# Block 2's decay: masked copies ahead of weight splits and convolutions, subtractions on GpSimd, exponentials over half tiles

## The reference, cut to what matters

```python
f = lb + (1.0 - lb) * jax.nn.sigmoid(f_raw)
log_f = jnp.log(f)
k = 1.0 - f
...
G = jnp.cumsum(lfc, axis=2)
diff = G[:, :, :, None, :] - G[:, :, None, :, :]
decay = jnp.where(mask, jnp.exp(jnp.minimum(diff, 0.0)), 0.0)
scores = jnp.einsum('bhtk,bhsk,bhtsk->bhts', qc, kc, decay)
```

## Time and profile before

| | us |
|---|---|
| median of 3 runs | 2746.95 (2746.0, 2746.95, 2749.92) |
| span of the profiled execution, first to last instruction | 2750.0 |
| PE busy in the span | 2545.7 (93%) |
| DVE busy | 1340.7 (49%) |
| ACT busy | 914.7 (33%) |
| GpSimd busy | 230.3 (8%) |

### The profile page before, as it was taken

The page is one execution under the profiler, slowest core; times in us unless marked ns, Lnnn a source line. Parts: engine busy times, 40 slices in busy tenths (PEclk is TensorE's granted clock), DMA queues, the critical chain, the costliest instruction groups (busy, mean ns, idle before and its releaser), DMA issues. The chain is left out here.

```text
span 2750.0 us, 39357 instructions
## 1 busy us (share of the span) xinstructions
PE 2545.7 (93%) x16728; PEld 1799.5 (65%) x16728; DVE 1340.7 (49%) x1877; ACT 914.7 (33%) x1236; POOL 230.3 (8%) x160
## 2 busy tenths in 40 slices
PE   7979899998999899678999899999999999999998
PEld 6652333332333333277799799899799899897897
DVE  4541122211212222277777665756575665765755
ACT  4431111110111111144454444444344444425443
POOL 2000000000000000000000011253020100102300
PEclk9989999999999999887899999999999999989999
DMA  9668999999999999942355466455466466441462
GB/s 322 235 239 365 427 428 403 427 428 427 427 400 426 427 427 427 364 127 92 108 193 194 163 212 211 157 177 191 153 223 209 154 209 205 139 156 35 166 205 101
DMA packets 248701, 713.71 MB, mean 260 GB/s; under 512 B 12531, under 2 KB 186313, under 8 KB 223622
## 3 DMA queue, kind: packets, MB, share of 16 engines
q1 hardware_dynamic: 237136, 690.26, 65.7%
q10 hardware_dynamic: 9734, 17.02, 1.8%
q0 software_dynamic: 1648, 3.82, 0.4%
HBM read 710.01 MB, written 1.05 MB: 259 GB/s over the span
## 5 line engine op out<-in xcount | busy, mean ns | idle before, releaser
L365 DVE TENSOR_TENSOR lo<-ring,hi 128x2048 fp32r<-128x2048 f32 x251 | 597.4, 2384 | 298.9 <-ACT hi L356 298.8
L356 ACT ACTIVATE hi<-ring 128x2048 fp32r<-128x2048 f32 x251 | 476.3, 1900 | 151.1 <-PE bank L653 116.2
L2014 PE MATMUL bank<-expert,xg 128*64 128x512 f32 x1664 | 393.7, 612 | 43.4 <-DMA expert<-in_w_mlp 42.2
L423 PE MATMUL bank<-x_hi,hi 128*128 128x256 f32 x1568 | 367.3, 279 | 0.0
L423 PE MATMUL bank<-x_lo,hi 128*128 128x256 f32 x1568 | 364.6, 278 | 0.0
L423 PEld LDWEIGHTS bank<-x_hi,hi 128*128 128x128 f32 x1568 | 295.1, 188 | 3.2 <-issue 1.6
L423 PEld LDWEIGHTS bank<-x_lo,hi 128*128 128x128 f32 x1568 | 294.9, 188 | 2.5 <-issue 1.0
L2014 PEld LDWEIGHTS bank<-expert,xg 128*64 128x64 f32 x1664 | 115.7, 139 | 257.8 <-issue 228.1
L2141 DVE TENSOR_TENSOR acc<-bank,acc 128x512 f32<-128x512 f32 x104 | 64.6, 684 | 329.4 <-PE bank L2122 329.4
L428 PE MATMUL bank<-x_hi,lo 128*128 128x256 f32 x1568 | 195.8, 277 | 0.6 <-DVE lo L365 0.6
L2097 PE MATMUL bank<-expert,aT 128*64 128x512 f32 x832 | 186.7, 600 | 5.6 <-DMA expert<-in_w_mlp 4.5
(11 more groups left out here) (650 smaller groups left out, 3776.8 us busy)
## 6 DMA issues: line engine op xcount, KB each, us to landing
expert<-in_w_mlp SPq DMA_DIRECT2D x192, 2048.0 KB, 18.8
ring<-in_l_ffn_w_in SPq DMA_DIRECT2D x88, 1024.0 KB, 5.0
ring<-in_l_ffn_w_out SPq DMA_DIRECT2D x44, 1024.0 KB, 4.8
ring<-in_w_ada SPq DMA_DIRECT2D x24, 1024.0 KB, 6.9
ring<-in_l_gm_w_in SPq DMA_DIRECT2D x24, 1024.0 KB, 5.2
ring<-in_ffn_w_up SPq DMA_DIRECT2D x22, 1024.0 KB, 5.0
ring<-in_w_in SPq DMA_DIRECT2D x21, 1024.0 KB, 7.2
ring<-in_l_gm_w_out SPq DMA_DIRECT2D x12, 1024.0 KB, 4.7
```

Of the source, the lines that this page charges most:

```text
L356: e.activation(k.half("hi", u), k.slot(j), ACT.Copy).then_inc(*k.up("hi_done"))
L365: e.tensor_tensor(k.half("lo", u), k.slot(k.units[u][0]), k.half("hi", u).bitcast(F32), SUB).then_inc(*k.up("lo_done"))
L423: e.matmul(o, l, r, start=fresh, stop=False, skip_group_check=True)
L2014: i = e.matmul(banks[n][j][h * CAP:(h + 1) * CAP, :], x, W[:, (2 * h + j) * 512:(2 * h + j + 1) * 512], start=c == 0, stop=False, skip_gro ...
```

## The change

- DVE's iteration li is now: the two multiplications for level li, copies(li-1), `between_dve(li)`.
- The eight differences are taken on GpSimd, by a new function `decay_less_pool`. The one of level li may start when DVE is through with the multiplications of level li-2, whose `hgE` buffer it takes.
- ACT makes exp(-x) of the lower half and exp(x) of the upper half of every block, two instructions over 384 columns each, with no absolute value ahead of them.
- Before a tanh at level 6, ACT waits for its own instructions.

```diff
+def decay_less_pool(k, e, nm, n):
+
+    e.wait_ge(*k.dve(nm, "sums"))
+    for li in range(1, 9):
+        h = LEVELS[li]
+        nb, r, v = decay_views(k, nm, n, h)
+        P, E = v(k.t[f"{nm}P{r}"]), v(k.t[f"{nm}E{li % 2}"])
+        if li >= 3:
+            e.wait_ge(*k.dve(nm, "level", li - 2))
+        e.tensor_tensor(E, P, P[:, :, h - 1:h].to_broadcast([128, nb, 2 * h]), SUB).then_inc(*k.POOL(nm, "E", li))
...
-    e.wait_ge(*k.dve())
+    k.mark("dve_done", nm, "sums")
     for li in range(10):
-        if li < 8:
-            h = LEVELS[li + 1]
-            nb, r, v = decay_views(k, nm, n, h)
-            P, E = v(k.t[f"{nm}P{r}"]), v(k.t[f"{nm}E{(li + 1) % 2}"])
-            e.wait_ge(*k.dve())
-            e.tensor_tensor(E, P, P[:, :, h - 1:h].to_broadcast([128, nb, 2 * h]), SUB).then_inc(*k.DVE(nm, "E", li + 1))
         if 0 < li < 9:
...
-        if between and li < 9:
-            between(k, e, li)
         if li > 0:
...
                     e.copy_predicated(out[:, :, 0:3:2, :], mask, bank[:, 0:w * 256].rearrange("p (c b s) -> p c b s", c=w, b=2)).then_inc(*k.DVE(*key, frees=key))
...
+        if between and li < 9:
+            between(k, e, li)
...
+def decay_act(k, e, nm, n, between=None):
     for li in range(9):
         if li < 8:
-            E = k.t[f"{nm}E{(li + 1) % 2}"]
-            e.wait_ge(*k.dve(nm, "E", li + 1))
-            e.activation(E, E, ACT.Abs).then_inc(*k.ACT())
-            e.wait_ge(*k.act())
-            e.activation(E, E, ACT.Exp, scale=-1.0).then_inc(*k.ACT(nm, "E", li + 1))
+            h = LEVELS[li + 1]
+            E = decay_views(k, nm, n, h)[2](k.t[f"{nm}E{(li + 1) % 2}"])
+            e.wait_ge(*k.pool(nm, "E", li + 1))
+            e.activation(E[:, :, 0:h], E[:, :, 0:h], ACT.Exp, scale=-1.0).then_inc(*k.ACT())
+            e.activation(E[:, :, h:2 * h], E[:, :, h:2 * h], ACT.Exp).then_inc(*k.ACT(nm, "E", li + 1))
```

More of the change, by code:

```diff
@@ L813, in decay_dve @@
                     e.copy_predicated(out[:, :, 0:3:2, :], mask, bank[:, 0:w * 256].rearrange("p (c b s) -> p c b s", c=w, b=2)).then_inc(*k.DVE(*key, frees=key))
-def decay_act(k, e, nm, between=None):
+        if between and li < 9:
+            between(k, e, li)
+def decay_act(k, e, nm, n, between=None):
     for li in range(9):
         if li < 8:
-            E = k.t[f"{nm}E{(li + 1) % 2}"]
-            e.wait_ge(*k.dve(nm, "E", li + 1))
-            e.activation(E, E, ACT.Abs).then_inc(*k.ACT())
-            e.wait_ge(*k.act())
-            e.activation(E, E, ACT.Exp, scale=-1.0).then_inc(*k.ACT(nm, "E", li + 1))
+            h = LEVELS[li + 1]
[3 more added lines that the diff above has]
+            e.activation(E[:, :, h:2 * h], E[:, :, h:2 * h], ACT.Exp).then_inc(*k.ACT(nm, "E", li + 1))
         if between:
@@ L2533, in block2_act @@
     z_unit_act(k, e, 4)
-    decay_act(k, e, "hg", between_act)
+    decay_act(k, e, "hg", 3, between_act)
     for c in range(3):
@@ L2578, in between_act @@
     elif li == 6:
+        e.wait_ge(*k.act())
         e.activation(t["gth"], t["z"][:, 15:18, :], ACT.Tanh, scale=0.5).then_inc(*k.ACT("hg", "g"))
@@ L3911, in program_pool @@
     decay_pool(k, e, "hg", k.t["hS"])
+    decay_less_pool(k, e, "hg", 3)
     for n in ("mix2", "fin2"):
```

## The result

The changed kernel takes 2729.35 us as the median of 4 runs (2724.34 to 2735.28), the kernel before 2748.43 (2746.0 to 2752.16, 4 runs). The ratio is 0.9927 with a 95% interval of 0.9911 to 0.9943: it is faster, by 19.1 us or 0.7%. The forecast was 19 us faster, 2728 us, in a range of 2723 to 2736. That the two differences agree to 0.1 us is partly luck: the interval of the ratio stands for anything from 15.7 to 24.5 us, and the levels, for which the sum was made, gained 2 us more than the sum. The profiled execution of the changed kernel has a span of 2727.6 us and took 2729.38.

The account below looks back on a forecast made before the run. It took PE's stalls in the decay levels, waiting on DVE and ACT, and the slow clock as the bound; 8.9 + 6.1 + 3.7 = 18.7, say 19 us, took 2746.95 to 2728 us, range 2723 to 2736.

Parts of the forecast that it names:

- z10: PE unit in the levels: with no stall before it, keeps 2.4 GHz and takes 8.2 us instead of 14.3, 6.1 gained.
- The first term: PE from the start of the levels to z10: z10 starts 8.9 us earlier, net of new waits and slow clock.
- the wait before scores(2): PE at level 2: waits 2.1 us for DVE's multiplications, which stand behind a weight unit and the convolution.
- the slow clock in scores(2): PE at level 2: clock falls after the wait, so scores(2) take 3.9 us instead of 2.1, 1.8 lost.
- The clock at level 2: PE after the 2.1 us wait: clock falls, costing 1.8 us in scores(2) and 1.5 in z8.
- the fall seen after 1.18 us: PE in the kernel before: clock fell right after the 1.18 us stall in scores(4), taken as evidence against the rival.
- the rival: Clock stays up at level 2 because the 2.1 us wait is short: 3.3 us less lost, 2725 us; chance 0.14.
- the stall in scores(4): PE: the 1.18 us stall, right after which the clock fell and z10 took 14.3 us, would be gone.
- The median row: GpSimd subtract-like row of 128x1024, median 4.32 us beside DVE work; scaled to 3.2 us as the difference's upper end.
- the copies would not be hit: DVE's masked copies read PSUM and one mask, so GpSimd's differences cost them nothing; up to 1.8 us for copies(0) otherwise.
- The chain behind z10: ACT and DVE from z10's end to scores(7): 3.7 us less, from absolute value 0.75, difference 0.95, copies 2.0.
- The wait that ACT got: ACT's wait for its own instructions, after scores(7): costs 0.1 us at most, covered by its wait for the scans.

Follow-up runs that it names:

- spread: Changed kernel with the convolution's first chunk left at level 1 and the other two moved to level 2; 2724.27 us, levels 69.1 us.
- stall4: Changed kernel with one added PE wait, ahead of the last group of scores(4), for the exponentials of level 6; 2735.64 us, levels 79.3 us.
- no_move: Changed kernel with the order of the copies put back as in the kernel before; 2738.69 us, levels 81.4 us.
- pool_twice: Changed kernel with each difference taken twice on GpSimd, a wait between; 2732.71 us, levels 75.0 us.
- move_halves: Changed kernel with the differences left on DVE, keeping the new copy order and half exponentials; 2730.9 us, levels 74.9 us.
- move_only: Kernel before with only the order changed, masked copies ahead of the weight unit and convolution; 2734.56 us, levels 80.4 us.
- tail: Changed kernel with ACT's square root and GELU moved behind the exponentials of level 7 and the next unit's rounding; 2723.51 us, levels 69.1 us.

## Why the prediction was right, point by point

**The sum.** It was 8.9 + 6.1 + 3.7 = 18.7 us in the levels. In the profiles, each counted from its own end of the scans, z10 starts 11.1 us earlier (40.3 instead of 51.4), takes 5.9 less (8.4 instead of 14.3), and from its end to scores(7) it is 3.65 less (16.2 instead of 19.9): 20.7. From scores(7) to `hS` both kernels take 7.65.

**The first term was 2.2 us too small**, in three parts that nearly explain it. scores(2) ran at 2.4 GHz after all (2.1 us, 3.9 were booked), which is 1.8. z7 started 12.5 us earlier instead of 11.65, as the slow clock at z5 ended 1.7 us sooner in this execution, which is worth half of that. Against that the wait before scores(2) was 2.70 us instead of 2.1, for the same reason: PE came earlier, DVE did not. So the term that was mis-sized is the slow clock in scores(2), booked at 1.8 us and absent.

**The clock at level 2.** I had weighed the rule of the Trainium skill (TensorE: Matmul & The Clock Gate, Part 1), by which a wait of this size keeps the clock, against the fall seen after 1.18 us, and went with the row. The clock did fall, and z8 lost its 1.5 us, but scores(2) did not. So the rival had one half of its 3.3 us. spread, where the wait is gone, kept the clock, but stall4 kept it as well, behind a wait of 2.54 us. From the start of scores(2) to that of scores(3) it takes 10.3 us in stall4 and in the three profiles with the convolution spread, and 11.9 us in each of the five profiles with waits from 2.45 to 4.02 us. Such a wait mostly costs 1.6 us of slow clock and sometimes nothing; its length alone does not settle it, and what does stays open.

**z10.** The cause that I named, the stall in scores(4), was only argued from the order of events, and "right after" was not exact: z10 ran at full pace for its first 1.7 us. stall4 shows that such a stall is enough, with all else as in the changed kernel.

**GpSimd.** The difference took 1.48 us; I had taken 1.8, with 1.4 as one end. The median row was the wrong neighbour for it, as it stood beside DVE work with two SBUF inputs; beside L365 in no_move the same difference took 3.49 us, near my upper end of 3.2. That the copies would not be hit was right, and pool_twice shows it with differences that outlast them (2.00 us again). It shows as well what a collision on the shared way to SBUF costs, 1.0 us on L365. The advice of the Trainium skill (GPSIMD Engine Reference, 4.1 Engine selection) to leave elementwise work on VectorE would have cost time here: GpSimd is 0.5 us slower with each difference, and the levels are 2.4 us shorter than in move_halves, since only the first one is waited for. Of the 2.4 us, 1.4 come ahead of z10 and 1.0 behind it.

**The chain behind z10** was 3.65 us shorter where 3.7 were booked, and its three terms hold one by one: 1.8 us for the copies (move_only against before, 2.0 booked), 0.9 for the exponentials (move_halves against move_only, 0.75) and 1.0 for the difference (changed against move_halves, 0.95). tail shows that the two table loads and functions that I had named hold 3.4 us of what is left.

**The wait that ACT got** is not on the path: ACT waits 4.3 us for the scans a few rows later.

**Where I was wrong** in the experiments was no_move: I had a stall in scores(4) that did not come, as I had moved copies(3) by the convolution's rows and forgot the difference taken off each level of DVE.

## What to carry to other kernels

Where engines run fixed programs and PSUM banks rotate, put what frees a bank ahead of everything that only fills time: here a 2 us copy behind 8 us of other work cost PE 9.6 us. A short stall of PE can cost more than its length, since the unit behind it may run at half clock (6.4 us behind a stall of 1.46 us in stall4, but nothing behind one of 2.54 us in the same execution): look at the granted clock before and after each stall, and at how long the same unit takes elsewhere in the trace. To compare versions that differ by 0.2%, compare the changed stretch between two fixed events in the profiles, as it repeated to 0.1 and 0.6 us in the two kernels that were profiled twice, whose spans differed by 12.1 and 5.1 us.

## What the runs showed of the hardware that I had not expected

- After the stall of 2.70 us before scores(2), the clock stayed at 2.4 GHz for the whole of scores(2) and fell to 1.2 GHz when z8 began. After 4.70 us (move_only) it was at 1.2 GHz for all of scores(2), 3.94 us. After 2.54 us (stall4) it did not fall at all.
- z10 began at 2.4 GHz, fell to 1.2 after 1.7 us (before) and 1.0 us (stall4), and never returned in the rest of its 14.3 and 14.8 us with PE busy throughout, while other units that began slow (z7 and z11 before, z8 in the changed kernel) returned after 3 to 4 us. z10 is the unit with matmuls of 128 columns among those of 256; no run here shows whether that is the reason.
- After a stall of 7.5 to 9.0 us ahead of z5, scores(1) began 7.7 to 9.2 us after the scans in the executions in which they did not wait for DVE, so the return of the clock alone moves the start of the levels by over 1 us.
- GpSimd subtracts 768 columns in 1.46 to 1.55 us, whether the broadcast operand changes every 2 columns or every 256.
- GpSimd and a DVE instruction with two inputs from SBUF went one after the other where they met. The one that started second took longer by about what the first still had to run: the difference in no_move 3.49 us instead of 1.48 (L365 began 0.14 us ahead of it), L365 in pool_twice 3.25 instead of 2.27 (the difference ended 1.1 us into it). Masked copies from PSUM beside a difference took their usual 2.0 us.
